# First expert pair and last expert visit of a mixture-of-experts stage: four pieces of VectorE's order and one unread TensorE product

## The chip, the cores and the metric

One Trainium2 chip, one of its NeuronCores. The metric is the device time of one launch in microseconds (us). Of the kernel before there are three timed runs, with a median of 2537.95 us (2536.84 to 2539.97 us), and one profiled execution of its own.

TensorE (PE in the profile) multiplies, VectorE (DVE) and ScalarE (ACT) do elementwise work, GpSimd (POOL) does small elementwise work and indirect transfers, and SyncE (SP) issues the weight stream.

## The reference, cut to what matters

Two networks run behind each other on 256 tokens of width 1024: an even layer and an odd layer, then a second block of two layers. The change lies in the odd layer's mixture of experts:

```python
def moe_swiglu(xn, router, wg, wu, wd):
    logits = (xt @ router).astype(F32)
    topv, topi = lax.top_k(logits, TOP_K)               # TOP_K = 2
    gates = jax.nn.softmax(topv, axis=-1)
    combine = jnp.sum(jax.nn.one_hot(topi, N_EXPERTS) * gates[..., None], axis=1)
    for e in range(N_EXPERTS):                          # 8 experts, EXPERT_DIM 3584
        y = y + combine[:, e:e + 1] * swiglu(xt, wg[e], wu[e], wd[e])
```

`xt` is the RMS-normed input, 256 x 1024; `wg`, `wu` are 1024 x 3584 and `wd` is 3584 x 1024 for each expert. All is float32.

## The kernel before, in words

**Visits and pairs.** An expert is computed for the tokens that chose it, up to 128 of them, in one *visit*. In this run there are eight visits. A visit goes through its expert in 14 *pairs* of 128 hidden columns each. The weights of a pair stream from HBM into a ring of four slots: slots r and r+1 (r = 0 or 2) hold the gate and up part (two transfers of 1024 KB) and the down part (two of 512 KB) of one pair.

**Split weights.** Every product is made of three products of rounded parts: hi x hi, hi x lo and lo x hi. So each pair's weights are cut into six *pieces* q0 to q5 of 128 x 1024, four of gate and up and two of down. ScalarE writes the hi part of a piece (L2355, `moe_split_act`) and VectorE the lo part, source less hi (L2528, `moe_split_lo`). In the very first pair GpSimd does the lo parts of q4 and q5 (same line, on POOL). Piece q covers the k-steps 2q and 2q+1 of the gate and up product.

**One pair on TensorE.** `moe_gate_up_pe` runs eight k-steps of three products of 128x512 (L2109, L2110, L2111). Then `moe_down_pe` of the pair before runs twelve products (L2140 to L2142), and `moe_transpose_pe` turns the hidden rows (L2118). ScalarE takes the SiLU (L2361), VectorE multiplies it with the up half (`moe_hidden_dve`, L2630, which the transposes wait for), ScalarE and VectorE split the turned rows (L2377, L2634).

**The first pair.** It is written out by hand, since its input is gathered at the same time. TensorE gathers the expert's rows by a product with a 0/1 matrix (`moe_gather_pe`, L2085), in two halves of four k-steps, and signals each. For each half VectorE scales the gathered rows by the norm's gain from PSUM into SBUF (`moe_xe_rows_dve`, L2512), ScalarE rounds them to hi (`moe_xe_act`, L2338), and VectorE subtracts to get lo (`moe_xe_lo_dve`, L2519), with a signal `moe_xe` that TensorE waits for: 1 ahead of k-step 0, 2 ahead of k-step 4. TensorE also waits for q1's lo part ahead of k-step 2 (`moe_w_lo`), and ahead of k-step 4 for `e_used[0]`, which VectorE raises with q3. The latter signal is also what SyncE waits for before it loads the gate and up part of pair 2 into the same slots; q5's signal does this for the down part. GpSimd's order here is: the row copy to HBM, nine small operations on gate weights (L2569 to L2575), q4 and q5, and then some seventy small ones for the later visits (L2584 and on).

VectorE's order in this pair (`moe_first_dve`, L2612) is q1, q2, rows of half 0, rows of half 1, lo of half 0, q3, lo of half 1, then q0 and q1 of the next pair, the hidden product, and so on. ScalarE's order (`moe_act`) is q3, hi of half 0, q4, hi of half 1, q5, then the next pair's pieces.

TensorE's order around the gather (`moe_pe`, L2286 on) is: one *unread product* (`idle_pe`: a 128x512 product of constants, in two passes, into a bank that nobody reads), the wait for the normed rows, the gather, the load of the number of visits into a register, and the first gate and up product.

**The last visit.** Every visit but the last writes its weighted output rows to a table in HBM. In the last one GpSimd fetches them back by indirect transfer (L2456): two transfers at once (for each token its row of one visit, in two blocks of 128 tokens), and two more once VectorE has added the first ones. VectorE adds half a block (128x512) at a time (`moe_back_dve`, L2643), at the end of a pair's work: parts 0 to 3 in pairs 4 to 7 and parts 4 to 7 in pairs 9 to 12. Part 0 and part 4 first wait for the transfers of their group. In this visit TensorE also turns context rows (L2129), and ScalarE evicts them (L2375).

```python
        def idle_pe(pe, n, bank=7, cols=512):
            for _ in range(n):
                pe.matmul(psum[:, bank, 0:cols], ident, cst("mask4")[:, 0:cols], start=True, stop=True)
```

Of the kernel before, what the change touches and what calls it, by code (L numbers as in the profile page):

```python
# [103 lines left out]
def program(nc, x_in, ctx_in, pos_in, pack_in, const_in, band_in, bias_in, stream_in, out):  # L104
# [10 lines left out]
    with ctx:  # L115
# [59 lines left out]
        def cst(name):  # L175
            o, n = CONST[name]
            return const[:, o:o + n]
# [1835 lines left out]
        xe_hi, xe_lo = [parts(27648 + D * i, D, "p (k s) -> p k s", k=KD) for i in range(2)]  # L2013
        AHEAD, POOL_LRU = 4, 3
        INDEX_AT, GATHER_AT = 6, 8
        BACK_AT, BACK0 = (4, 5, 6, 7, 9, 10, 11, 12), 96
        x_rows = nc.dram_tensor("x_rows", (NT * P, D), f32).ap()
        BACK_NONE = (MAX_VISITS - 1) * P
        y_rows = nc.dram_tensor("y_rows", (BACK_NONE + 1, D), f32).ap()
# [53 lines left out]
        def moe_more(eng):  # L2073

            eng.wait_ge(sem("moe_plan"), 1)
            return eng.value_load(plan_i[0:1, 12:13], min_val=N_EXP - 1, max_val=MAX_VISITS - 1)
# [11 lines left out]
        def moe_gather_pe(pe, v):  # L2088
            pe.wait_ge(sem("moe_pick"), v + 1)
            for half in range(2):  # L2090
                for c in range(4):
                    k = 4 * half + c
                    ins = moe_pick_rows_pe(pe, psum[:, 4 + half, c * CAP:(c + 1) * CAP], k)
                ins.then_inc(sem("moe_gather"), 1)
# [177 lines left out]
        def moe_pe(pe):  # L2272
            pe.sem_inc(sem("moe_dn"), AHEAD)

            idle_pe(pe, 1)
            route_turn_pe(pe, 1)
            pe.wait_ge(sem("moe_choice"), 1)
            pe.matmul(psum[:, 7, 0:8], before, sel[:, :, 0], start=True, stop=True)
            pe.matmul(psum[:, 7, 8:24].rearrange("p (a e) -> p a e", a=2), cst("ones"),
                      sel[:, :, 0].unsqueeze(1).to_broadcast([P, 2, N_EXP]), start=True, stop=False)  # L2280
            route_logits_pe(pe, 1)
            idle_pe(pe, 1, 5)
            pe.wait_ge(sem("moe_choice"), 2)
            pe.matmul(psum[:, 7, 8:16], before, sel[:, :, 1], start=False, stop=False)
            pe.matmul(psum[:, 7, 16:24], cst("ones"), sel[:, :, 1], start=False, stop=True).then_inc(sem("moe_routed"), 1)
            idle_pe(pe, 1, 6)  # L2286
            pe.wait_ge(sem("norm_xn"), 5)
            moe_gather_pe(pe, 0)
            n_more = moe_more(pe)
            moe_gate_up_pe(pe, moe_at(0, 0), True)  # L2290
            moe_transpose_pe(pe, moe_at(0, 0), 0)
            moe_gate_up_pe(pe, moe_at(0, 1))
            pe.wait_ge(sem("moe_tables"), 1)
            for j in range(NT):
                pe.matmul(psum[:, 0, 0:1], pick[:, j, :].bitcast(f32), token_of[:, j, 2:3],
                          start=(j == 0), stop=(j == NT - 1))

            def visit(v, more):
                for p in range(PAIRS):
                    if p > 0 and (p + 1 < PAIRS or more):  # L2300
                        if p + 1 == PAIRS:
                            pe.wait_ge(sem("moe_xe"), v + 3)
                        moe_gate_up_pe(pe, moe_at(v, p + 1))
                    moe_down_pe(pe, moe_at(v, p), p)
                    if more and p + 1 == INDEX_AT:
                        pe.wait_ge(sem("moe_pick"), v + 2)
                    if more and p + 1 == GATHER_AT:
                        pe.wait_ge(sem("pool_out"), POOL_LRU + v + 1)
                    if not more and p + 1 == CTX_AT:
                        pe.wait_ge(sem("ctx_xn"), 3)  # L2310
                    if p + 1 < PAIRS:
                        moe_transpose_pe(pe, moe_at(v, p + 1), p + 1, chunks_at(p + 1) if more else (),
                                         () if more else ctx_parts_at(p + 1), more)
                if more:
                    moe_transpose_pe(pe, moe_at(v, PAIRS), 0)
                    moe_gate_up_pe(pe, moe_at(v, PAIRS + 1))
                else:
                    l0_first_pe(pe)
                pe.wait_ge(sem("moe_out_act"), 2 * v + 2)
                if more:  # L2320
                    return
                for j in range(NT):
                    for hf in range(2):
                        pe.matmul(psum[:, 2 * j + hf, :], giveT[:, j, :], oute_hi[:, hf, :], start=True, stop=False)
                pe.wait_ge(sem("moe_out_dve"), 1)
                for j in range(NT):
                    for hf in range(2):
                        ins = pe.matmul(psum[:, 2 * j + hf, :], giveT[:, j, :], oute_lo[hf], start=False, stop=True)
                    ins.then_inc(sem("moe_sum"), 1)

            with pe.Fori(0, n_more) as v:
                visit(v, True)
            visit(n_more, False)
# [173 lines left out]
        def moe_xe_rows_dve(dve, half):  # L2507

            ks = slice(4 * half, 4 * half + 4)
            dve.wait_ge(sem("moe_gather"), half + 1)  # L2510
            gain = vec("o_ln_ffn", 4 * half, 4).unsqueeze(2).to_broadcast([P, 4, CAP])
            step(dve, dve.tensor_tensor(xe[:, ks, :], psum[:, 4 + half, :].rearrange("p (c s) -> p c s", c=4), gain, MUL),  # L2512
                 "moe_xe_own")
# [98 lines left out]
        def moe_first_dve(dve):  # L2612

            own, nxt = moe_at(0, 0), moe_at(0, 1)
            moe_split_lo(dve, own, 0, 1, 3)
            moe_xe_rows_dve(dve, 0)
            moe_xe_rows_dve(dve, 1)
            moe_xe_lo_dve(dve, 0)
            moe_split_lo(dve, own, 0, 3, 4)
            moe_xe_lo_dve(dve, 1)  # L2620
            moe_split_lo(dve, nxt, 1, 0, 2)
            moe_hidden_dve(dve, own)
            moe_split_lo(dve, nxt, 1, 2, 4)
            dve.wait_ge(sem("moe_h_hi"), 1)
            moe_hidden_lo_dve(dve)
            moe_split_lo(dve, nxt, 1, 4, 6)
# [20 lines left out]
        def moe_dve(dve):  # L2647
            route_dve(dve)
            moe_first_dve(dve)

            def visit(v, more, first=False):
                for p in range(1, PAIRS):
                    if not more and p + 1 == PAIRS:
                        l0_lo_dve(dve, 1, slice(0, KD), 1)
                    moe_stage_dve(dve, moe_at(v, p), moe_at(v, p + 1) if more or p + 1 < PAIRS else None, p,
                                  xe_next=v if more and p + 1 == PAIRS else None, more=more,
                                  gate=psum[:, 0, 0:1] if first else gate_next)
                    if p == 1 and not more:
                        for j in range(NT):
                            ins = dve.tensor_scalar(xn[:, j, :], xc_tm[:, j, :], ctx_rstd[:, j:j + 1], None, MUL)  # L2660
                        ins.then_inc(sem("ctx_xn"), 1)
                    if more and p in (3, 4):
                        moe_gate_dve(dve, v + 1, p - 3)
                        moe_pick_dve(dve, v + 1, p - 3)
                    if not more and p in BACK_AT:
                        moe_back_dve(dve, v, BACK_AT.index(p))
                    if first and p == PAIRS - 1:
                        dve.wait_ge(sem("pool_out"), POOL_LRU)
                        dve.wait_ge(sem("ctx_xn"), 1)
                        dve.tensor_reduce(back_f[:, 0:NT], back_at.rearrange("p (v j) -> p j v", j=NT), AX.X, MIN)\  # L2670
                           .then_inc(sem("ctx_xn"), 1)
                if more:
                    moe_stage_dve(dve, moe_at(v, PAIRS), moe_at(v, PAIRS + 1), 0)
                else:
                    l0_piece_dve(dve, 0)
                    l0_piece_dve(dve, 1)
                    moe_out_dve(dve, v)

            visit(0, True, True)
            n_more = moe_more(dve)  # L2680
            with dve.Fori(1, n_more) as v:
                visit(v, True)
            visit(n_more, False)
            for j in range(NT):
                dve.wait_ge(sem("moe_sum"), j + 1)
                step(dve, dve.tensor_tensor(x_tm[:, j, :], x_tm[:, j, :],
                                            psum[:, 2 * j:2 * j + 2, :].rearrange("p b n -> p (b n)"), ADD), "moe_x")
            dve.wait_ge(sem("x_squares"), 4 * NT)
# [1537 lines left out]
```

## Time and profile before

| | |
|---|---|
| median of 3 timed runs | 2537.95 us |
| the profiled execution's own time | 2546.52 us |
| its span | 2544.80 us |
| TensorE busy | 2477.8 us, 97% |
| VectorE busy | 1924.3 us, 76% |
| ScalarE busy | 1502.8 us, 59% |
| GpSimd busy | 162.2 us, 6% |
| first pair, from the gather's start to the first transposes | 593.06 to 607.49 us of the span |
| last visit | about 1446 to 1562 us of the span |

The profiled execution's own time is its span and 1.72 us around it. It is 8.57 us (0.34%) above the median of the timed runs. Times in a row are us from the span's start, and the duration behind it is that of the group of equal instructions (x2 is two of them). An engine's next instruction is sometimes shown to start some 0.08 us before the last one ends; sums therefore go from end to end.

### The profile page before, as it was taken

The page shows a single profiled execution, that of the slowest core. Times are in us where ns is not written, and L with a number is a line of the kernel's source. Part 1 is how long each engine was busy: PE and PEld are TensorE (multiplying, and loading weights), DVE is VectorE, ACT ScalarE, POOL GpSimd, SP SyncE. Part 2 cuts the span into 40 slices and gives each one's busy share as a digit, 9 for nine tenths or more (in the row PEclk, how much of TensorE's full clock was granted, in tenths as well). Part 3 has the DMA queues.
Part 4 walks back from the last instruction along what each step waited for, and adds up shares of the span by engine and source line. Part 5 has one row for each costly group of instructions (what it writes and reads, how often), then busy time and mean ns, then how long its engine had stood idle before and what let it go on. Part 6 is the DMA issues. An engine that isn't in the chain of part 4 may idle for free.

```text
span 2544.8 us, 41865 instructions
## 1 busy us (share of the span) xinstructions
PE 2477.8 (97%) x15881; PEld 2103.1 (83%) x15881; DVE 1924.3 (76%) x2668; ACT 1502.8 (59%) x2186; POOL 162.2 (6%) x144
## 2 busy tenths in 40 slices
PE   8899999989999999999999999999999999999998
PEld 7677999857888888888888888857999999876998
DVE  7857555768999999999999987876656655688655
ACT  5614334456888888888888885392443443257432
POOL 0101000006500010000100100000000000010000
PEclk9999999999999999999999999999999999999999
DMA  6647543577999999999999994203554552232551
GB/s 263 248 174 294 196 175 123 222 329 287 385 374 372 385 372 384 365 393 367 393 364 389 370 387 190 116 1 136 194 191 162 197 188 100 100 133 77 221 190 50
DMA packets 93052, 627.17 MB, mean 246 GB/s; under 512 B 10496, under 2 KB 10752, under 8 KB 42880
## 3 DMA queue, kind: packets, MB, share of 16 engines
q1 hardware_dynamic: 88992, 609.17, 62.1%
q0 software_dynamic: 3360, 12.06, 1.2%
q10 hardware_dynamic: 576, 4.19, 0.5%
q8 instruction: 89, 1.46, 0.2%
q14 instruction: 35, 0.29, 0.0%
HBM read 618.04 MB, written 7.34 MB: 246 GB/s over the span
## 4 chain that ended last, share of the span: by engine, by line
PE 82%; DVE 9%; DMA 4%; ACT 4%; issue 1%; SPq 0%; POOL 0%; DVEq 0%; ACTq 0%
PE psum L2109 7%; PE psum L2111 7%; PE psum L2110 7%; PE psum L436 7%; PE psum L438 7%; PE psum L437 7%; DMA ring<-stream_dram 4%; PE psum L2140 4%; PE psum L2142 4%; PE psum L2141 4%; PE psum L451 3%; PE psum L452 3%; PE psum L453 3%; DVE r_high L2528 1%; PE psum L2731 1%
## 5 line engine op out<-in xcount | busy, mean ns | idle before, releaser
L2528 DVE TENSOR_TENSOR r_high<-ring,r_high 128x1024 fp32r<-128x1024 f32 x670 | 796.5, 1230 | 53.7 <-ACT r_high L2355 43.4
L2355 ACT ACTIVATE r_high<-ring 128x1024 fp32r<-128x1024 f32 x672 | 700.8, 1061 | 74.4 <-PE psum L2111 42.9
L436 PE MATMUL psum<-r_low,r_high 128*128 128x256 f32 x1408 | 400.1, 284 | 1.5 <-DVE r_high L526 0.9
L438 PE MATMUL psum<-r_low,r_high 128*128 128x256 f32 x1408 | 398.5, 283 | 0.0
L2109 PE MATMUL psum<-r_high 128*128 128x512 f32 x896 | 360.0, 402 | 1.9 <-DVE r_high L2519 1.9
L2111 PE MATMUL psum<-r_high 128*128 128x512 f32 x896 | 350.4, 391 | 0.0
L2110 PE MATMUL psum<-r_high 128*128 128x512 f32 x896 | 349.9, 391 | 0.0
L526 DVE TENSOR_TENSOR r_high<-ring,r_high 128x1024 fp32r<-128x1024 f32 x263 | 305.9, 1217 | 9.3 <-ACT r_high L485 9.0
L437 PE MATMUL psum<-r_high 128*128 128x256 f32 x1056 | 298.8, 283 | 0.0
L499 ACT ACTIVATE arena<-psum 128x256 f32<-128x256 f32 x88 | 33.8, 384 | 435.8 <-PE psum L438 433.0
L436 PEld LDWEIGHTS psum<-r_low,r_high 128*128 128x128 f32 x1408 | 270.1, 192 | 6.9 <-DVE r_high L3313 1.5
L537 DVE TENSOR_TENSOR arena<-arena,psum 128x256 f32<-128x256 f32 x88 | 37.1, 421 | 308.7 <-ACT arena L499 308.5
L438 PEld LDWEIGHTS psum<-r_low,r_high 128*128 128x128 f32 x1408 | 269.9, 192 | 0.0
L437 PEld LDWEIGHTS psum<-r_high 128*128 128x128 f32 x1056 | 202.5, 192 | 3.2 <-issue 0.9
L2111 PEld LDWEIGHTS psum<-r_high 128*128 128x128 f32 x896 | 168.6, 188 | 36.4
L2109 PEld LDWEIGHTS psum<-r_high 128*128 128x128 f32 x896 | 168.6, 188 | 33.9 <-DVE r_high L2519 2.1
L2110 PEld LDWEIGHTS psum<-r_high 128*128 128x128 f32 x896 | 169.1, 189 | 32.0
L485 ACT ACTIVATE r_high<-ring 128x1024 fp32r<-128x1024 f32 x176 | 176.1, 1052 | 15.2 <-DMA ring<-stream_dram 10.0
L2140 PE MATMUL psum<-r_high 128*128 128x512 f32 x448 | 174.5, 390 | 0.9 <-DVE r_high L2634 0.9
L2142 PE MATMUL psum<-r_high 128*128 128x512 f32 x448 | 174.8, 390 | 0.0
L2141 PE MATMUL psum<-r_high 128*128 128x512 f32 x448 | 174.3, 389 | 0.0
L451 PE MATMUL psum<-r_high 128*128 128x512 f32 x352 | 139.2, 396 | 0.0
(682 smaller groups left out, 4539.5 us busy)
## 6 DMA issues: line engine op xcount, KB each, us to landing
ring<-stream_dram SPq DMA_DIRECT2D x160, 1536.0 KB, 6.5
ring<-stream_dram SPq DMA_DIRECT2D x224, 1024.0 KB, 7.0
ring<-stream_dram SPq DMA_DIRECT2D x224, 512.0 KB, 7.0
y_rows<-arena POOLq DMA_DIRECT2D x7, 512.0 KB, 9.2
arena<-bias_dram ACTq DMA_DIRECT2D x2, 1024.0 KB, 7.8
pack<-pack_dram SPq DMA_DIRECT2D x1, 1664.0 KB, 17.0
y_rows<-const POOLq DMA_DIRECT2D x3, 512.0 KB, 10.8
const<-const_dram SPq DMA_DIRECT2D x1, 1060.0 KB, 13.5
```

The costliest lines, as they stand in the source:

```text
L436: pe.matmul(dst, hi, f["x_hi"][:, k, :], start=(k == 0 and part == 0), stop=False)
L437: pe.matmul(dst, hi, f["x_lo"][:, k, :], start=False, stop=False)
L438: ins = pe.matmul(dst, lo, f["x_hi"][:, k, :], start=False, stop=(k == KD - 1 and part == 1))
L526: ins = dve.tensor_tensor(lo, slot_of[r][:, o:o + D], hi.bitcast(f32), SUB)
L2109: pe.matmul(dst, xe_hi[:, k, :], hi, start=(k == 0), stop=False)
L2110: pe.matmul(dst, xe_hi[:, k, :], lo, start=False, stop=False)
L2111: ins = pe.matmul(dst, xe_lo[:, k, :], hi, start=False, stop=(k == KD - 1))
L2140: pe.matmul(dst, eh_hi[:, h, :], hi, start=(p + h == 0), stop=False)
L2141: pe.matmul(dst, eh_hi[:, h, :], lo, start=False, stop=False)
L2142: ins = pe.matmul(dst, eh_lo[:, h, :], hi, start=False, stop=(p == PAIRS - 1 and h == 1))
L2355: act.activation(dst, src, ACT.Copy).then_inc(sem("moe_w_hi"), 1)
L2528: ins = eng.tensor_tensor(lo, src, hi.bitcast(f32), SUB)
```

## The change

Three edits. On TensorE, one more unread product (into bank 0) behind the gather. On VectorE, another order in the first pair: q1, rows of half 0, lo of half 0, rows of half 1, q2, lo of half 1, q3. In the last visit, part 4 of the returned rows is added in pair 10 together with part 5, in place of pair 9; the wait for the second group's transfers goes with it.

```diff
@@ -2013,7 +2013,7 @@
-        BACK_AT, BACK0 = (4, 5, 6, 7, 9, 10, 11, 12), 96
+        BACK_AT, BACK0 = {4: (0,), 5: (1,), 6: (2,), 7: (3,), 10: (4, 5), 11: (6,), 12: (7,)}, 96
@@ -2286,6 +2286,7 @@
             idle_pe(pe, 1, 6)
             pe.wait_ge(sem("norm_xn"), 5)
             moe_gather_pe(pe, 0)
+            idle_pe(pe, 1, 0)
             n_more = moe_more(pe)
             moe_gate_up_pe(pe, moe_at(0, 0), True)
@@ -2612,12 +2613,13 @@
             own, nxt = moe_at(0, 0), moe_at(0, 1)
-            moe_split_lo(dve, own, 0, 1, 3)
+            moe_split_lo(dve, own, 0, 1, 2)
             moe_xe_rows_dve(dve, 0)
+            moe_xe_lo_dve(dve, 0)
             moe_xe_rows_dve(dve, 1)
-            moe_xe_lo_dve(dve, 0)
+            moe_split_lo(dve, own, 0, 2, 3)
+            moe_xe_lo_dve(dve, 1)
             moe_split_lo(dve, own, 0, 3, 4)
-            moe_xe_lo_dve(dve, 1)
             moe_split_lo(dve, nxt, 1, 0, 2)
             moe_hidden_dve(dve, own)
@@ -2662,8 +2664,8 @@
-                    if not more and p in BACK_AT:
-                        moe_back_dve(dve, v, BACK_AT.index(p))
+                    for i in BACK_AT.get(p, ()) if not more else ():
+                        moe_back_dve(dve, v, i)
```

## Rows read from the trace of the kernel before

**Rows 1.** Windows, all engines: stretch and length, PE, PEld, DVE, ACT, POOL busy; clock; DMA.

```profile
900.00:1000.00 100.00, 100.00 (x457) 82.53 (x456) 93.14 (x98) 84.64 (x105) 7.16 (x3) 1.00 0.97 378
```

**Rows 2.** The chain that ended last, 594 to 608 us: start, us, what.

```profile
594.24 2.40 DVE r_high L2528 x2
...
598.01 0.69 DVE r_high L2519
598.70 1.14 DVE r_high L2528
599.84 2.78 DVE r_high L2519
602.62 4.48 DVE r_high L2528 x2
...
607.49 0.44 PE psum L2118 x2
```

**Rows 3.** Timeline of GpSimd: the operations beside VectorE's, in two stretches.

```profile
596.75 0.19 POOL L2575 COPY pack<-pack 128x2 f32<-128x2 f32 x1
...
1456.30 3.37 POOL L2487 TENSOR_TENSOR arena<-arena 128x2 f32<-128x2 f32 x1 [10.28 <-DVE arena L2660]
```

**Rows 4.** Line L2528 alone, 600.5 to 603.5 us: durations ns min/median/max, first and last start.

```profile
L2528 POOL TENSOR_TENSOR r_high<-ring,r_high x2: 2843/2955/3067, 599.0 to 602.0; 128x1024 fp32r<-128x1024 f32 x2
```

**Rows 5.** Timeline of VectorE: the rows' scaling, and the q0 to q2 that GpSimd's 3.37 us overlap.

```profile
596.57 1.40 DVE L2512 TENSOR_TENSOR arena<-psum,pack 128x512 f32<-128x512 f32 x2
...
1456.13 3.48 DVE L2528 TENSOR_TENSOR r_high<-ring,r_high 128x1024 fp32r<-128x1024 f32 x3
```

**Rows 6.** Timeline of ScalarE in the first pair.

```profile
595.30 1.06 ACT L2355 ACTIVATE r_high<-ring 128x1024 fp32r<-128x1024 f32 x1 [1.74 <-issue]
597.28 0.63 ACT L2338 ACTIVATE r_high<-arena 128x512 fp32r<-128x512 f32 x1 [0.92 <-DVE arena L2512]
597.81 1.04 ACT L2355 ACTIVATE r_high<-ring 128x1024 fp32r<-128x1024 f32 x1
...
606.15 0.38 ACT L2361 ACTIVATE arena<-psum 128x256 f32<-128x256 f32 x1 [0.30 <-PE psum L2111]
```

**Rows 7.** Timeline of TensorE: unread product, gather, first products of k-steps 0 and 4.

```profile
591.84 1.10 PE L384 MATMUL psum<-const 128*128 128x512 f32 x2
593.06 3.81 PE L2085 MATMUL psum<-r_mid,arena 128*128 128x128 f32 x32
598.76 0.50 PE L2109 MATMUL psum<-r_high 128*128 128x512 f32 x1 [1.89 <-DVE r_high L2519]
...
603.20 0.40 PE L2109 MATMUL psum<-r_high 128*128 128x512 f32 x1
```

**Rows 8.** Windows, TensorE alone: stretch and length, busy (x), granted clock, DMA share, GB/s.

```profile
599.00:600.00 1.00, 1.00 (x4) 0.74 0.00 0
...
602.00:603.00 1.00, 1.00 (x4) 0.55 0.88 352
603.00:606.00 3.00, 3.00 (x14) 1.00 1.02 429
...
1705.00:1712.00 7.00, 6.29 (x24) 0.53 0.01 2
```

**Rows 9.** Timeline of SyncE: the gate and up load of pair 2.

```profile
600.03 0.88 SPq L3904 DMA_DIRECT2D ring<-stream_dram  x2
```

**Rows 10.** Timeline of the last visit: second fetch, part 4, hidden product of pair 11, its turn.

```profile
1510.55 1.97 POOL L2456 DMA_INDIRECT arena<-y_rows,arena  x1 [0.30 <-issue]
...
1526.00 0.68 DVE L2643 TENSOR_TENSOR x<-x,arena 128x512 f32<-128x512 f32 x1
...
1538.89 0.41 DVE L2630 TENSOR_TENSOR arena<-arena,psum 128x256 f32<-128x256 f32 x1
...
1539.68 0.38 PE L2118 MATMUL psum<-const,arena 128*128 128x128 f32 x2
```

**Rows 11.** Transfers that touch the table of returned rows, 1440 to 1560 us.

```profile
DMA to landing us min/median/max: 8.4/9.5/10.8
```

## The prediction

> **What bounds the kernel now.** I read the windows of a visit first. TensorE is busy for the whole of a 100 us stretch in the middle, at full clock, VectorE for 93 us and the DMA engines for 97% [rows 1]. So in the visits TensorE sets the pace. A load is issued only when VectorE or GpSimd frees its slots, so it moves with the compute: a microsecond lost at the head of the first visit is hardly won back later.
>
> The chain that ended last shows where the head is different. From 594.24 to 607.4 us it lies on VectorE alone: q1 and q2, the rows, a lo part, q3, the second lo part, q0 and q1 of the next pair, the hidden product, and then the turn on TensorE at 607.49 [rows 2]. TensorE had idled 1.89 us behind the gather, then ran its first twelve products slowly [rows 7]: the granted clock is 0.74 over 599 to 600 us, 0.55 over 602 to 603 and 1.00 behind it, so it stood at 1.2 in place of 2.4 GHz from about 599.5 to 602.9 [rows 8]. These twelve took 4.44 us (598.76 to 603.20). It looks like the thing to win. It isn't, since k-step 4 also needs q3 and the second lo part, which ended at 602.62 [rows 2]. At full clock TensorE would have stood there at about 601.5 and waited until 602.7: all that the low clock cost is some 0.5 us.
>
> What made VectorE late is GpSimd. The second lo part is 128x512, as is the first, which took 0.69 us, yet it took 2.87 us and ended at 602.62; it lay beside GpSimd's q4, which shows 3.07 us from 599.0. GpSimd's q5 (2.84 us from 602.0) lies beside q0 of the next pair, and two pieces that take 2.4 us elsewhere took 4.48 us [rows 2, 4]. The pattern is strict alternation: q3 ends at 599.84, then q4 runs (2.23 us, to 602.07), then the lo part (0.55 us), then q5 (2.25 us, to 604.88), then q0. One waits while the other runs. The rows' scaling, which reads PSUM, blocks nothing: a GpSimd copy beside it took 0.19 us [rows 3, 5]. The Trainium skill, SBUF — State Buffer, in the section on the two separate sides, states the rule: a VectorE operation with two SBUF inputs and a GpSimd operation that reads SBUF hold one port pair in turns, and the other fully blocks. By that rule the new order meets both GpSimd pieces ahead of k-step 4.
>
> **The VectorE order, step by step.** VectorE starts q1 at 594.24 as before and ends it at 595.44 (half of 2.40). Rows of half 0 take 0.70 (half of 1.40), to 596.14 [rows 2, 5]; the gather's first half was done by 595.1 (half of its 3.81 us, plus its drain) [rows 7]. ScalarE's q3 is unchanged and ends at 596.36; its hi of half 0 then takes 0.63, to 596.99, and its q4 0.95 to 1.04 more, to about 597.95, which is 0.9 us sooner than the 598.85 of before [rows 6]. VectorE waits 0.85 us for the hi part and does lo of half 0 by 597.68. TensorE can start k-step 0 at about 597.75 in place of 598.76: a gain of 1.0 us at the start. Rows of half 1 end at 598.36.
>
> GpSimd's q4 needs ScalarE's q4 and followed it by 0.15 us before, so it starts at 598.1, while VectorE scales rows and holds nothing. It runs 2.23 us, to 600.33. VectorE now has three subtractions ahead of k-step 4 (q2, lo of half 1, q3) where it had, once q4 had come, one. By the alternation of the rows: q2 to 601.45 (1.14 long), GpSimd's q5 to 603.70, lo of half 1 to 604.25 (0.55), q3 to 605.4 (1.14) [rows 2, 4]. So k-step 4 starts at 605.45, where it started at 603.20 [rows 7]: 2.25 us later.
>
> From there the SiLU starts 2.95 us after k-step 4 (606.15 less 603.20), at 608.40, and ends at 608.78 [rows 6]. VectorE has done q0 and q1 of the next pair by then (605.4 plus 2.3 is 607.7), so it no longer holds up the hidden product as it did before by about 0.5 us. That product takes 0.4, and the turn starts at 609.3, in place of 607.49 [rows 2]. **Term 1: +1.8 us.** If GpSimd blocked nothing, q3 would end at 601.3, k-step 4 would follow k-step 3 at 600.5 to 601.3, and the turn would come at 604.5 or so: -3 us. These are the two ends.
>
> **The unread product.** Two passes behind the gather, on TensorE from 596.87. The one ahead of the gather took 1.10 us from start to end, with its second pass free for the next instruction sooner [rows 7], so it ends at about the 597.75 at which k-step 0 is released; its own cost is 0 to 0.2 us and is covered by the wait for k-step 4 in any case. It fills the idle 1.89 us, and I take it that the clock stays up for the first twelve products. They end at 600.5 or so. That is worth nothing, as the wait for 605.45 comes next: an idle of 4.9 us, longer than the 1.89 us that was followed by the low clock before. I expect the low clock there, over the second twelve products. Half the time spent low is lost: 4.44 us against 2.75 before shows 1.7 lost in the 3.4 us at 1.2 GHz. There is also a longer low stretch in the trace, nearly all of 1705 to 1712 us (0.53) [rows 8]. The bounds are 0 (the clock is back when k-step 4 starts) and 2.75 us (all twelve slow); I take 1.7, one stretch of the shorter kind. **Term 2: +1.7 us.**
>
> **The slots.** q3's signal lets SyncE issue the gate and up load of pair 2, which it did at 600.03 [rows 9]. It now comes at 605.45. Relative to TensorE it is 1.9 to 3.6 us later. The pieces of pair 2 are wanted only for the product behind the whole of pair 1 (twenty-four products, over 5 us), so I cost this at 0. If that cover is gone, ScalarE waits at q0 of pair 2.
>
> **The last visit.** The second group's transfers are issued by 1510.55 and a bit, and the slowest takes 10.8 us, so they have landed at about 1521.4 [rows 10, 11]. Part 4 comes at 1526.00: no wait there now, so no wait goes. Its 0.68 us moves from pair 9 to pair 10. In pair 10 VectorE's hidden product ends at 1539.30 and TensorE turns at 1539.68, directly behind its products [rows 10]: 0.38 us to spare, against one more addition of 0.61 (0.68 less the overlap). **Term 3: +0.25 us.** Between 0 (the turn isn't held) and 0.6 us. In pair 9 nothing is won if VectorE waits for the weights; 0.2 us at most if not.
>
> **The sum.** 1.8 + 1.7 + 0.25 = 3.75 us. Against the profiled execution (2546.52 us, its span of 2544.80 and 1.72 around it) that makes 2550.3 us; that execution is 8.57 us above the median of the timed runs, and the same difference on the median, 2537.95, makes **2541.7 us**. What a measurement can tell from no change is about 0.2%, 5.1 us. So the forecast is slower in the trace and no change by that bound.
>
> **The rivals.** (A) *GpSimd misses its turn.* The trace has a case: a tiny operation shows 3.37 us from 1456.30, beside three subtractions in a row, q0 to q2 of a pair [rows 3, 5]. If q5 waits in this way until q3 is done, VectorE runs q2, lo and q3 from 600.33 to 603.2, k-step 4 starts where it did, and q5 then delays q0 and q1 (hidden product at 607.9). With 0 to 1.4 us for the clock, +1 us in all: 2539 us. For it: the one case. Against it: GpSimd got in after both of VectorE's operations in the first pair. Chance 17%.
>
> (B) *The new order is met by no lock*, or GpSimd's q4 comes in a gap: -3 us, 2535 us. For it: nothing in this stretch; q4 would have to be released later. Against it: the two 2.8 to 3.1 us rows. Chance 10%.
>
> (C) *Slower beyond the bound.* The late refill of the slots decides it: the load of pair 2 starts 5.4 us later than before while the down load waits behind it, so 3 MB are asked for at once. If ScalarE's q0 of pair 2 then comes more than 5 us late, TensorE waits. With all twelve products slow (2.75) and the wait (1 us or more) the sum is 1.8 + 2.75 + 0.25 + 1 = 5.8 us or more: 2543.8 us. It decides from the point at which the idle ahead of k-step 4 is over 5 us. Chance 13%.
>
> The forecast has the other 60%. That an edit doesn't do what it says is possible for the product alone: if the clock falls in spite of it, the first twelve products end at 602.9 and are still ahead of 605.4, so the time stays.
>
> **The numbers.** Time 2541.7. The range reaches from 2536.0 (most of B left out) to 2545.0 (C, its low end, and 1 us of spread of the runs). Faster by over 0.2% needs more than B gives: 0.04. Slower by over 0.2% is C and the top of the forecast's own bounds (1.8 + 2.75 + 0.6 is 5.15): 0.16. Within: 0.80.
>
> **What would show it.** Right: GpSimd's q4 starting near 598.1 and VectorE's q2 some 3.1 us long in place of 1.2; q3 ending at 605 to 606; TensorE idle over 4 us ahead of k-step 4, with a clock of 0.5 behind it; the first turn near 611. In the last visit, an idle of 0.2 to 0.3 us ahead of pair 11's turn. Wrong: q3 ending before 603, or a first turn ahead of 607.5.

## The result, and the profile after

The changed kernel takes 2542.4 us (median of 14 runs, 2541.14 to 2547.86), the kernel before 2538.77 us (14 runs beside them, 2536.56 to 2541.91). The ratio is 1.0017, with a 95% interval of 1.0009 to 1.0025: slower by 2.3 to 6.3 us, 3.6 us in the medians. The ratio is within the 0.2% that was called no change; the interval reaches to 0.25%.

The profiled execution's own time was 2541.14 us, 5.4 us *under* the profiled one of before. That isn't the change, for 4.8 us of it lie ahead of the gather. In it the gather starts at 588.27 us, in the one of before at 593.06 us, ahead of everything that the change touches; over the twelve profiles of this study that moment lies anywhere between 586.8 and 593.1 us. The profile of before is also longer where the change can't reach: from the last visit's sum to the end of the span it takes 980.3 us, the changed one 978.0. So times of the head are given from here on from the start of the gather's first product. The head of the kernel before agrees there with that of a kernel that differs only in the last visit to 0.02 us; with the new order, k-step 0 lies between 4.53 and 4.83 us in kernels that are alike up to there, so that differences of 0.3 us or less are not read as an effect.

The page of the changed kernel, and the windows of a visit, look as before: TensorE sets the pace of the visits at full clock, as in [rows 1].

```profile
span 2539.4 us, 41869 instructions
PE 2470.3 (97%) x15883; PEld 2099.7 (83%) x15883; DVE 1925.0 (76%) x2668; ACT 1503.8 (59%) x2186; POOL 152.5 (6%) x144
```

```profile
900.00:1000.00 100.00, 100.00 (x458) 82.53 (x457) 93.12 (x99) 84.31 (x106) 4.80 (x3) 1.00 0.97 379
```

The chain that ended last, through the first pair (start us, us, what). It answers to [rows 2]. In this kernel L2513 scales rows, L2520 makes the lo part of the rows, L2529 that of a piece, and L2632 the hidden product.

```profile
592.70 0.69 DVE arena L2513
593.42 3.15 DVE r_high L2529
596.57 2.75 DVE r_high L2520
599.32 1.15 DVE r_high L2529
600.61 0.77 PE psum L2109
...
605.70 0.39 ACT arena L2362
606.11 0.43 DVE arena L2632
606.59 0.44 PE psum L2118 x2
```

The first L2529 is q2, the second q3. q2 took 3.15 us in place of 1.2 and the lo part of half 1 took 2.75: both have a GpSimd piece in them. Before, only the lo part had one ahead of k-step 4. The same line on both engines (durations in ns, min/median/max; first and last start):

```profile
L2529 POOL TENSOR_TENSOR r_high<-ring,r_high x2: 2406/2866/3327, 593.1 to 595.4; 128x1024 fp32r<-128x1024 f32 x2
L2529 DVE TENSOR_TENSOR r_high<-ring,r_high x2: 1219/2182/3146, 593.4 to 599.2; 128x1024 fp32r<-128x1024 f32 x2
```

GpSimd's q4 began at 593.1, 4.8 us behind the gather's start, since ScalarE's q4 (the third row below) no longer stands behind a wait for the rows. Before it began at 599.0, 5.9 us behind it [rows 4, 6]. ScalarE's timeline:

```profile
590.39 1.06 ACT L2356 ACTIVATE r_high<-ring 128x1024 fp32r<-128x1024 f32 x1 [1.62 <-issue]
591.36 0.63 ACT L2339 ACTIVATE r_high<-arena 128x512 fp32r<-128x512 f32 x1
591.90 1.04 ACT L2356 ACTIVATE r_high<-ring 128x1024 fp32r<-128x1024 f32 x1
```

TensorE's timeline: the new unread product, k-step 4 with the idle time ahead of it, and the first turn; it answers to [rows 7].

```profile
591.91 1.02 PE L384 MATMUL psum<-const 128*128 128x512 f32 x2
...
600.61 0.77 PE L2109 MATMUL psum<-r_high 128*128 128x512 f32 x1 [4.75 <-DVE r_high L2529]
...
606.59 0.44 PE L2118 MATMUL psum<-const,arena 128*128 128x128 f32 x2 [0.93 <-DVE arena L2632]
```

The windows of TensorE alone (stretch and length, busy, granted clock, DMA share, GB/s), as in [rows 8]:

```profile
594.00:598.00 4.00, 1.86 (x9) 1.00 0.00 0
598.00:601.00 3.00, 0.39 (x1) 0.54 0.00 0
601.00:605.00 4.00, 4.00 (x10) 0.50 0.84 276
605.00:606.00 1.00, 0.66 (x3) 0.98 1.05 442
```

The first four k-steps run at 2.4 GHz. Then TensorE idles for 4.75 us, the clock falls inside that time, at about 598.2, and k-steps 4 to 7 run at 1.2 GHz up to 605.0. SyncE's loads of pair 2, which waited for q3 [rows 9], came both at once:

```profile
600.66 0.88 SPq L3906 DMA_DIRECT2D ring<-stream_dram  x2
601.72 1.04 SPq L3910 DMA_DIRECT2D ring<-stream_dram  x2
```

In the last visit the two additions of pair 10 and the turn of pair 11 (timeline; compare [rows 10]):

```profile
1531.53 1.29 DVE L2645 TENSOR_TENSOR x<-x,arena 128x512 f32<-128x512 f32 x2
...
1536.14 0.41 DVE L2632 TENSOR_TENSOR arena<-arena,psum 128x256 f32<-128x256 f32 x1
...
1536.61 0.44 PE L2118 MATMUL psum<-const,arena 128*128 128x128 f32 x2
```

The turn is held for VectorE: 0.13 us between the end of the last product (1536.48) and 1536.61.

### The profile page after: what moved, and what is told of

The parts are those of the page before. It is cut to its first block, busy times and chain, and to the rows that moved or that the text cites. A ratio compares the mean times of both kernels' runs of the same rounds, so it can differ in the third digit from the quotient of the medians.

```text
span 2539.4 us, 41869 instructions
## 1 busy us (share of the span) xinstructions
PE 2470.3 (97%) x15883; PEld 2099.7 (83%) x15883; DVE 1925.0 (76%) x2668; ACT 1503.8 (59%) x2186; POOL 152.5 (6%) x144
## 4 chain that ended last, share of the span: by engine, by line
PE 85%; DVE 8%; ACT 4%; DMA 2%; issue 1%; POOL 0%; ACTq 0%; DVEq 0%; SPq 0%
PE psum L2109 8%; PE psum L2111 8%; PE psum L2110 8%; PE psum L436 7%; PE psum L438 7%; PE psum L437 7%; PE psum L2142 4%; PE psum L2140 4%; PE psum L2141 4%; PE psum L451 3%; PE psum L452 3%; PE psum L453 3%; DMA ring<-stream_dram 2%; PE psum L2118 1%; PE psum L2733 1%
## 5 line engine op out<-in xcount | busy, mean ns | idle before, releaser
L2529 DVE TENSOR_TENSOR r_high<-ring,r_high 128x1024 fp32r<-128x1024 f32 x670 | 797.0, 1230 | 50.8 <-ACT r_high L2356 40.9
```

The lines of the kernel that those rows point to most:

```text
L2529: ins = eng.tensor_tensor(lo, src, hi.bitcast(f32), SUB)
```

## The experiments

Each kernel of the experiments has eleven timed runs and one profile. An interval is some 0.09% to either side, 2.3 us, as large as most of the effects looked for, so the moments of the profile say more than the medians. The table gives these moments, in us behind the start of the gather's first product, and in the last two columns the time from the start of the last visit's part 3 to the last product of the visit's sum, and the ratio to before with its interval.

| kernel | k-step 0 | k-step 4 | last k-step's last product | first turn | second turn | part 3 to the sum | ratio |
|---|---|---|---|---|---|---|---|
| before | 5.70 | 10.15 | 12.67 | 14.43 | 23.42 | 56.85 | |
| changed | 4.57 | 12.34 | 17.00 | 18.32 | 27.32 | 55.84 | 1.0017 (1.0009 to 1.0025) |
| order only | 4.75 | 12.52 | 17.35 | 18.70 | 27.70 | 55.47 | 1.0012 (1.0003 to 1.0021) |
| product only | 5.70 | 9.65 | 12.28 | 14.46 | 23.46 | 55.47 | 0.9998 (0.9989 to 1.0007) |
| part 4 only | 5.70 | 10.14 | 12.68 | 14.44 | 23.41 | 55.80 | 0.9998 (0.9989 to 1.0007) |
| wait filled, nine | 4.83 | 15.04 | 17.98 | 19.30 | 28.29 | 56.67 | 1.0018 (1.0009 to 1.0027) |
| wait filled, five | 4.56 | 12.33 | 14.93 | 16.25 | 25.23 | 55.84 | 1.0001 (0.9992 to 1.0010) |
| GpSimd held | 4.53 | 8.21 | 10.83 | 12.93 | 23.43 | 55.83 | 0.9997 (0.9988 to 1.0006) |
| all on VectorE, new order | 4.71 | 8.39 | 11.01 | 12.33 | 22.08 | 55.83 | 0.9994 (0.9985 to 1.0003) |
| all on VectorE, old order | 5.70 | 8.56 | 11.05 | 12.60 | 22.35 | 55.83 | 0.9994 (0.9985 to 1.0003) |
| the same, new order, part 4 in pair 9 | 4.56 | 8.25 | 10.87 | 12.18 | 21.93 | 56.22 | 0.9998 (0.9989 to 1.0007) |
| and q2 in VectorE's gap | 4.97 | 7.82 | 10.32 | 12.01 | 21.76 | 55.49 | 1.0002 (0.9993 to 1.0011) |

### The three edits one by one

**VectorE's order alone**, in the kernel before:

```diff
-            moe_split_lo(dve, own, 0, 1, 3)
+            moe_split_lo(dve, own, 0, 1, 2)
             moe_xe_rows_dve(dve, 0)
+            moe_xe_lo_dve(dve, 0)
             moe_xe_rows_dve(dve, 1)
-            moe_xe_lo_dve(dve, 0)
-            moe_split_lo(dve, own, 0, 3, 4)
+            moe_split_lo(dve, own, 0, 2, 3)
             moe_xe_lo_dve(dve, 1)
+            moe_split_lo(dve, own, 0, 3, 4)
```

> The kernel before with VectorE's new order alone (no unread product behind the gather, part 4 of the returned rows stays in pair 9). Theory (GpSimd's q4 and q5 both get in ahead of k-step 4): k-step 4 starts 12.3 us behind the gather's first product, in place of 10.15, and the first transposes 3.9 us later than before; with the low clock on k-steps 4 to 7 again. Time +3 to +4 us, ratio about 1.0014. The product should make no difference to these, since the first four k-steps are waited for in any case. Rival (the loss comes from the product or from the last visit): k-step 4 where it was, time within 1 us of before.

The median was 2541.06 us beside 2538.81. The turn came 4.27 us later than before. TensorE's timeline has the same wait as the changed kernel:

```profile
600.78 0.77 PE L2109 MATMUL psum<-r_high 128*128 128x512 f32 x1 [4.75 <-DVE r_high L2528]
```

The order alone holds the loss. The product makes no difference beyond 0.4 us at the turn, of which 0.2 us are there at k-step 0 already. Nor was it the product that kept the first four k-steps fast. Without it, but with the new order, TensorE idles 0.94 us ahead of k-step 0 in place of 1.89, and the granted clock stays at 1.00 (a row of the timeline and a window):

```profile
593.01 0.50 PE L2109 MATMUL psum<-r_high 128*128 128x512 f32 x1 [0.94 <-DVE r_high L2519]
```

```profile
592.00:595.00 3.00, 2.06 (x10) 1.00 0.23 90
```

**The unread product alone:**

```diff
             moe_gather_pe(pe, 0)
+            idle_pe(pe, 1, 0)
             n_more = moe_more(pe)
```

> The kernel before with the unread product behind the gather alone. Theory (VectorE behind GpSimd's two pieces sets the first hidden product): the first four k-steps run at full clock, k-step 4 starts at most 0.5 us sooner (9.65 us behind the gather's start in place of 10.15), the first transposes at the same 14.4 us, time 0 to -0.5 us. Rival (the low clock is what costs): -1.7 us at the first transposes. Second rival: the product is too little and the stretch at 1.2 GHz is there as before.

2538.19 us beside 2538.81. The chain, and one window of TensorE:

```profile
595.46 2.81 DVE r_high L2520
598.27 4.48 DVE r_high L2529 x2
```

```profile
593.00:596.00 3.00, 1.97 (x8) 1.00 0.11 41
596.00:599.00 3.00, 2.07 (x10) 1.00 0.78 221
```

There is no stretch at 1.2 GHz any more. k-step 4 starts 0.50 us sooner, as forecast, and the turn comes at 14.46 us in place of 14.43. The timeline has the wait that took the place of the slow products, for VectorE's hidden product:

```profile
603.13 0.44 PE L2118 MATMUL psum<-const,arena 128*128 128x128 f32 x2 [1.80 <-DVE arena L2631]
```

**Part 4 in pair 10 alone:**

```diff
-        BACK_AT, BACK0 = (4, 5, 6, 7, 9, 10, 11, 12), 96
+        BACK_AT, BACK0 = {4: (0,), 5: (1,), 6: (2,), 7: (3,), 10: (4, 5), 11: (6,), 12: (7,)}, 96
...
-                    if not more and p in BACK_AT:
-                        moe_back_dve(dve, v, BACK_AT.index(p))
+                    for i in BACK_AT.get(p, ()) if not more else ():
+                        moe_back_dve(dve, v, i)
```

> The kernel before with part 4 of the returned rows in pair 10 alone. Theory: the head of the first visit as before; an idle of 0.1 to 0.3 us on TensorE ahead of pair 11's transposes; time 0 to +0.3 us. Rival (the move frees VectorE in pair 9 and lets a load start sooner): TensorE's idle in front of pair 9's transposes (0.87 us before) goes, time -0.5 to -1 us.

2538.91 us beside 2538.81; an idle of 0.13 us ahead of pair 11's turn. The price shows best across profiles. From part 3 to the sum there are 55.80 to 55.84 us in the six kernels that have the edit and no other stall, and 55.47 to 55.49 us in the three that don't have it: the edit costs 0.35 us. All of it lies at that turn. The idle time of 0.13 us is less than the delay, since an unhindered product is shown to start before the last one ends: from the last product ahead of the turn to the second behind it there are 1.02 us with the edit and 0.68 without.

The profiles of before, of "nine" and of "part 4 in pair 9" are outliers by a stall of TensorE of 0.87, 0.64 and 0.55 us, at the turn of pair 9 or 10. It comes in kernels of either kind, so the runs don't say that the edit avoids it. The rival saw such a stall in the profile of before and took it for its own. In all three it follows a late load: ScalarE waited for weights to land, 2.03 us in before (its timeline below), 1.79 in "nine" and 1.70 in "part 4 in pair 9", against 0.93 us at most behind part 3 in the other nine profiles, and VectorE then waited for ScalarE (1.87, 1.62 and 0.93 us).

```profile
1517.12 2.96 ACT L2355 ACTIVATE r_high<-ring 128x1024 fp32r<-128x1024 f32 x3 [2.03 <-DMA ring<-stream_dram]
```

Measured from product to product, the late turns delay TensorE by 1.33 us (two turns), 0.85 and 0.77 us. Less that, the three come to 55.52, 55.82 and 55.45 us: each with the kernels of its kind.

### Does the low clock on k-steps 4 to 7 cost?

The changed kernel, with unread products in TensorE's wait ahead of k-step 4:

```diff
             for k in range(KD):
+                if first and k == 4:
+                    idle_pe(pe, 9, 0)
                 if first and k % 4 == 0:
                     pe.wait_ge(sem("moe_xe"), k // 4 + 1)
```

> The changed kernel with nine more unread products between k-steps 3 and 4 of the first pair, which fill most of TensorE's 4.75 us there. Theory (the low clock on k-steps 4 to 7 is the second term): k-step 4 starts where it does in the changed kernel, the granted clock stays at 2.4 GHz, the SiLU starts 2.95 us behind k-step 4 in place of 5.1, the first transposes 2 us sooner than in the changed kernel and 1.8 us later than before; time +1.5 to +2 us on before. Rival (the clock is low there for another reason, or the twelve slow products lie beside VectorE's q0 and q1 anyway): transposes within 0.5 us of the changed kernel's.

2543.57 us beside 2538.81. This expectation was wrong in one point of its design: an unread product takes 0.83 to 0.88 us, two passes, not half of it, and nine of them end 2.7 us behind the point at which k-step 4 could start. So the turn came at 19.30 us, later than in the changed kernel and not 2 us sooner.

```profile
595.19 7.89 PE L384 MATMUL psum<-const 128*128 128x512 f32 x18
```

The clock did stay up: from k-step 4 to the last product there are 2.94 us in place of 4.66. The same with `idle_pe(pe, 5, 0)`, in both kernels with all lines behind it two numbers later:

> The changed kernel with five unread products (some 4.15 us by the 0.83 us that one took in the run with nine) between k-steps 3 and 4 of the first pair, so that they end ahead of VectorE's q3. Theory (the second term is the low clock on k-steps 4 to 7): k-step 4 starts at 12.3 us behind the gather's first product as in the changed kernel, the last k-step starts 2.6 us later in place of 4.7, the first transposes come at 16.2 to 16.4 us in place of 18.3 (before: 14.4), time +1.5 to +2 us on before. Rival (0.9 us of idle left ahead of k-step 4 is enough for the low clock): transposes at 18 us.

```profile
594.22 4.45 PE L384 MATMUL psum<-const 128*128 128x512 f32 x10
599.13 0.47 PE L2111 MATMUL psum<-r_high 128*128 128x512 f32 x1 [0.46 <-DVE r_high L2531]
603.05 0.44 PE L2120 MATMUL psum<-const,arena 128*128 128x128 f32 x2 [0.93 <-DVE arena L2634]
```

```profile
599.00:602.00 3.00, 2.87 (x12) 1.00 0.61 153
```

k-step 4 stands where it did (12.33 beside 12.34), the last product comes 2.60 us behind it in place of 4.66, and the turn at 16.25 us. This run divides the loss at the head in two: 1.8 us against before from VectorE's lateness, and 2.1 us from the low clock. The median is 2539.01 beside 2539.24 us; its interval, 0.9992 to 1.0010, holds a loss of 1.8 us as well as none.

### Is it GpSimd that makes VectorE late?

The changed kernel, with GpSimd held until VectorE's q3 is done:

```diff
             moe_weights_pool(pool)
+            pool.wait_ge(e_used[0], 1)
             moe_split_lo(pool, moe_at(0, 0), 0, 4, 6)
```

> The changed kernel in which GpSimd waits for VectorE's q3 (its signal to the slots) before it does q4 and q5. Theory (the two GpSimd pieces between VectorE's subtractions are the first term): VectorE's q2, lo of half 1 and q3 run behind each other, k-step 4 starts at 8.2 to 8.4 us behind the gather's start in place of 12.3, and the clock stays up; the two pieces then lie beside q0 and q1 of the next pair, so the first transposes come at 13.2 us or so (changed kernel 18.3, before 14.4), and k-step 4 of the second pair waits about 1 us for its q3. Time within 1 us of before. Rival (VectorE is late by its own work, not by GpSimd): k-step 4 still at 11 us or later.

2538.51 us beside 2539.24. VectorE's timeline, then GpSimd's:

```profile
597.86 1.23 DVE L2530 TENSOR_TENSOR r_high<-ring,r_high 128x1024 fp32r<-128x1024 f32 x1
599.01 0.68 DVE L2521 TENSOR_TENSOR r_high<-arena,r_high 128x512 fp32r<-128x512 f32 x1
599.61 5.70 DVE L2530 TENSOR_TENSOR r_high<-ring,r_high 128x1024 fp32r<-128x1024 f32 x3
```

```profile
600.96 6.60 POOL L2530 TENSOR_TENSOR r_high<-ring,r_high 128x1024 fp32r<-128x1024 f32 x2 [4.91 <-DVE r_high L2530]
```

q2 is back at 1.23 us and the lo part at 0.68, with the same instructions in the same order: only GpSimd's moment has moved. k-step 4 starts at 8.21 us, 4.1 us sooner. The blocking then falls on the next pair's pieces: TensorE waits 0.96 us for VectorE ahead of that pair's k-step 4, as forecast, and the second turn comes at 23.43 us, to 0.01 us where it is in the kernel before.

Then no pieces on GpSimd at all:

```diff
-            moe_split_lo(pool, moe_at(0, 0), 0, 4, 6)
...
             moe_split_lo(dve, nxt, 1, 0, 2)
+            moe_split_lo(dve, own, 0, 4, 5)
             moe_hidden_dve(dve, own)
             moe_split_lo(dve, nxt, 1, 2, 4)
+            moe_split_lo(dve, own, 0, 5, 6)
```

> The changed kernel in which VectorE does the lo parts of q4 (ahead of the hidden product) and q5 (behind the next pair's q3) itself and GpSimd none. VectorE loses 1.14 us a piece in place of the 2.25 us that it waits for GpSimd's. Theory: k-step 4 at 8.2 to 8.4 us, the first transposes at 12.1 us, 2.3 us ahead of before; VectorE is then the late one for the second pair's hidden product, which gives 1 us or more back; time 1 us under before (2537.8 beside 2538.8) and 4 to 5 us under the changed kernel. Rival (two more pieces on an engine that is 93% busy in the visits): a loss that grows over the first pairs, time at or over before's.

```profile
593.85 1.22 DVE L2528 TENSOR_TENSOR r_high<-ring,r_high 128x1024 fp32r<-128x1024 f32 x1
594.99 0.68 DVE L2519 TENSOR_TENSOR r_high<-arena,r_high 128x512 fp32r<-128x512 f32 x1
595.59 4.63 DVE L2528 TENSOR_TENSOR r_high<-ring,r_high 128x1024 fp32r<-128x1024 f32 x4
```

2537.59 us beside 2539.24. The four pieces from q3 on take 4.63 us, 1.16 each. The first turn is at 12.33 us, the second at 22.08: 2.1 us and 1.3 us ahead of before, so 0.8 us of the gain is gone by the second pair. TensorE's timeline shows what holds the second turn, as forecast:

```profile
600.89 0.44 PE L2118 MATMUL psum<-const,arena 128*128 128x128 f32 x2 [0.93 <-DVE arena L2633]
610.64 0.44 PE L2118 MATMUL psum<-const,arena 128*128 128x128 f32 x2 [0.59 <-DVE arena L2633]
```

The same kernel with VectorE's order of before in front (the diff of "order only", reversed):

> The same as the run with all pieces on VectorE (product behind the gather, part 4 in pair 10, VectorE does q4 and q5), but with VectorE's order of before in front of them. It shows what the new order is worth with GpSimd out of the way. Theory: k-step 0 one us later than with the new order (5.7 us behind the gather's start), k-step 4 at 8.5 us, transposes within 0.3 us of the new order's at 12.2 to 12.4 us, and less VectorE idle ahead of them, so the second pair is 0.8 us better: time the same within 1 us, or better. Rival (the new order pays once GpSimd is away): transposes 1 us later and time 1 us more than with the new order.

2537.04 us beside 2539.24. First turn 12.60, second 22.35: 0.27 us behind the new order at both. So the new order is worth some 0.3 us at most when GpSimd is out of the way, no more than heads of like code differ by. The part of the expectation that VectorE's wait would make the old order better in the second pair was wrong.

### A better version?

Both kernels with all pieces on VectorE lie under both originals in the medians (2537.59 and 2537.04 against 2539.24), but the intervals of 0.9985 to 1.0003 reach over 1. Against the changed kernel the difference is clear of the noise: its interval, 1.0009 to 1.0025, doesn't meet theirs, nor that of the kernel with GpSimd held (0.9988 to 1.0006). Two more tries, the first with the last visit's part 4 back in pair 9:

> The run with all pieces on VectorE in the new order, but part 4 of the returned rows back in pair 9. Theory (the last visit's edit costs 0.35 us, as the four kernels with it and the two without it show between part 3 and the visit's end): from part 3 to the end of the visit 55.5 us in place of 55.8; the 0.13 us idle ahead of pair 11's transposes goes; time 0.3 us less than that run, 1.5 to 2.5 us under before. Rival (the 0.35 us is the spread between profiles): 55.8 us again.

2537.85 beside 2538.23 us. It had 56.22 us from part 3 to the sum, with the stall in it; less the 0.77 us by which that delayed TensorE it is 55.45, as in the kernels without the edit, and there is no wait ahead of pair 11's turn. So the 0.35 us is the edit's price and no spread of the profiles. The second also fills VectorE's wait for ScalarE:

```diff
             moe_xe_rows_dve(dve, 0)
+            moe_split_lo(dve, own, 0, 2, 3)
             moe_xe_lo_dve(dve, 0)
             moe_xe_rows_dve(dve, 1)
-            moe_split_lo(dve, own, 0, 2, 3)
-            moe_xe_lo_dve(dve, 1)
             moe_split_lo(dve, own, 0, 3, 4)
+            moe_xe_lo_dve(dve, 1)
```

> The run with all pieces on VectorE and part 4 in pair 9, with VectorE's order q1, rows of half 0, q2, lo of half 0, rows of half 1, q3, lo of half 1: q2 in the 0.85 to 0.95 us in which VectorE waits for ScalarE's hi part. Theory: k-step 4 starts 0.7 us sooner (7.7 us behind the gather's start in place of 8.4), the first transposes at 11.6 us in place of 12.3, the second pair's at 21.4 to 22.1; time 0.3 to 0.7 us less than the other run of this call. Rival (VectorE is behind in the second pair whatever the head does): the second pair's transposes at 22.1 us as in that run and no gain.

```profile
593.98 0.68 DVE L2519 TENSOR_TENSOR r_high<-arena,r_high 128x512 fp32r<-128x512 f32 x1
595.40 3.51 DVE L2528 TENSOR_TENSOR r_high<-ring,r_high 128x1024 fp32r<-128x1024 f32 x3 [0.74 <-ACT r_high L2356]
```

2538.45 beside 2538.23 us. k-step 4 came 0.43 us sooner (7.82 beside 8.25, 0.7 expected) and the turns only 0.17 us sooner, less than such heads differ by: VectorE now waits 0.74 us for ScalarE's q0 of the next pair, one wait in the place of another. The head of this kernel is 1.7 us ahead of before at the second turn, yet its median isn't under it: a gain of this size is not resolved by these timings.

## Why the prediction was right, step by step

**VectorE's order: +1.8 us forecast, +1.82 us measured** (16.25 less 14.43, in the run with five products, which has no low clock). The working holds row by row: k-step 0 was to start 4.7 us behind the gather's start (4.57), k-step 4 at 12.4 (12.34), q2 to be about 3.1 us long (3.15), GpSimd's q4 to start at 5.0 us (4.8). The rule of the Trainium skill that was weighed there (SBUF — State Buffer, on the two separate sides of the memory) agrees: one holds the shared ports, the other fully blocks, and the held run shows it with GpSimd's moment as the only thing changed. That the turns are one each, where both engines have large pieces waiting, was read from two cases and came out so here. It isn't shown to be general: the small GpSimd operation of 3.37 us beside three subtractions [rows 3, 5] is in the changed kernel's profile too, and no run explains it.

**The unread product:** the clock did stay up for the first twelve products, but the reason given, that the product fills the idle time, wasn't needed: the kernel with the order alone kept it up too, with 0.94 us of idle. It changed nothing in the sum, where the product stood at 0.

**The low clock: +1.7 forecast, +2.07 measured** (18.32 less 16.25). This is the term that was mis-sized. I took one stretch of the shorter kind, 3.4 us, all of it on products. The stretch was 6.83 us long, of which 2.4 us fell on the idle time and 4.4 us on the products. The upper bound of 2.75 us held. The cost is shown by one profile beside another; the medians point the same way but don't resolve it.

**The last visit: +0.25 forecast, 0.35 us measured**, with an idle of 0.13 us seen ahead of the turn, where 0.2 to 0.3 us were forecast; the products around it are 0.35 us later all the same.

**The slots at 0:** right. The load came at 600.66, 12.4 us behind the gather's start in place of 7.0, and ScalarE shows no wait for it.

**The sum** was 3.75 us; the terms as measured make 1.82 + 2.07 + 0.35 = 4.2 us, and the median rose by 3.6. That the forecast of 2541.7 us lies 0.7 us from the measured 2542.4 is in part luck: each term was too small, 0.5 us in all, and the median of three runs that they were added to was 0.8 us under that of fourteen. Neither can be told apart from the spread of the runs.

Is the loss carried to the end, and not won back in the visits? Beside the product-only kernel, whose first turn is that of before, it is: the changed kernel is 3.86 us behind it at the first turn, 3.84 us at the write of the seventh visit's rows (855.37 beside 851.53 us behind the gather's start), and 4.48 us at the last visit's sum (973.19 beside 968.71), where the third edit's 0.35 us have come on top. Beside the profile of before it is less clear: 3.89 us behind at the first turn, 3.01 at the seventh write (852.36) and 1.78 at the sum (971.41). In the last step 1.33 us are before's own late turns of the last visit; the 0.9 us between the first turn and the seventh write are left open. So a profile carries a difference at the head to the end to within 1 us or so, besides such stalls.

**The rivals.** GpSimd missing its turn (A) didn't come: both pieces got in, and the kernels with the same order and GpSimd's pieces in their place have k-step 4 at 12.3 to 12.5 us (the one with nine products aside). No lock (B) fell with the held run, and its price of -3 us was too large as well: without GpSimd the first turn is 2.1 us ahead of before. k-step 4 could then start at 8.2 to 8.4 us, while the price was worked out from the early end of its own range, 7.4 to 8.2, and over a third of the gain is gone at the second pair. The late refill (C) didn't decide anything; no wait for the load is shown.

**A reading that held:** the low clock of the kernel before looked like 1.7 us to be won. I gave it 0.5 us at k-step 4; it was 0.50 us there and nothing at the turn, since VectorE's hidden product was behind its own GpSimd wait.

## What to carry to other kernels

Before an operation is moved forward on VectorE, look at what that releases on GpSimd: here ScalarE's q4 came 1.1 us sooner, GpSimd's piece started sooner with it, and three subtractions of VectorE had to take turns with two of GpSimd, where there had been one. A helper that blocks the helped engine costs it the helper's own time in waiting (2.25 us a piece against 1.14 for doing it), so it pays only where VectorE idles or does something that isn't blocked, as the scaling of rows from PSUM (seen here beside the start of q4 and beside small copies of 0.19 us). And a slow clock is worth what the next wait leaves of it: look for what TensorE waits for at the end of the slow stretch before paying to avoid it.

## What the runs showed of the hardware that I had not expected

- The low stretch after an idle of 4.75 us lasted 6.83 us (changed kernel and order only), after one of 1.89 us 3.41 us (before and part 4 only). Idles of 1.80 us (product only) and 1.72 us (GpSimd held) in front of a turn, with full work in front of them, were followed by none, and neither was one of 1.03 us behind the gather and the unread product, nor one of 0.94 us behind the gather alone (order only).
- An unread product of 128x512 float32 constants takes 0.83 to 0.88 us in a row (7.89 us for nine, 4.45 for five).
- The head of the visit is reproducible to 0.02 us with VectorE's old order and to 0.3 us with the new one, while the moment at which it starts differs by up to 6.3 us. The runs of one kernel spread over 5 us or more; if they differ as the profiles do, that comes at least in part from ahead of the visit, and a change in one stage is read more finely from the stage's own moments than from the medians.
- TensorE stalls of 0.5 to 0.9 us at pair 9 or 10 of the last visit came in three profiles of twelve, whatever the kernel. In each, ScalarE had waited 1.7 to 2.0 us for weights to land. What makes that load late in some executions is left open.
